# Value tiles 1 to 3 as three rounded products, with their upper and lower parts made by ScalarE, GpSimd and VectorE

## The reference, cut to what matters

```python
z = x @ w_in                                  # columns: pool 256, q 384, k 384, v 384, ssm 384
y_pool = pool_mixer(u_pool, ...)              # trailing means of 2, 4, 8, 16 tokens, then a small product
y_attn = chunk_attention(q, k, v, rel_bias)   # 6 heads of 64, softmax over own and previous chunks
y_ssm  = s5_mixer(u_ssm, ...)                 # state space, GELU, then y * sigmoid(y @ w_glu + b)
heads  = concat(rmsnorm(y_pool), rmsnorm(y_attn), rmsnorm(y_ssm))
h      = layer_norm(ALPHA * x + heads @ w_out)
x      = layer_norm(ALPHA * h + moe(h) + sigmoid(h @ w_ple_gate) * (p @ w_ple_proj))
```

## Time and profile before

| what | value |
|---|---|
| time of the kernel, median of 3 runs | 428.99 us (428.87 to 429.12) |
| time of the profiled execution | 429.05 us |
| its span in the trace | 427.3 us |
| PE, PEld, DVE, ACT, POOL busy | 413.3, 238.1, 255.4, 129.6, 93.6 us |
| mean granted TensorE clock | 0.993 |
| DMA, mean over the span | 240 GB/s |

### The profile page before, as it was taken

The page is one execution under the profiler, slowest core; times in us unless marked ns, Lnnn a source line. Parts: engine busy times, 40 slices in busy tenths (PEclk is TensorE's granted clock), DMA queues, the critical chain, the costliest instruction groups (busy, mean ns, idle before and its releaser), DMA issues.

```text
span 427.3 us, 5594 instructions
## 1 busy us (share of the span) xinstructions
PE 413.3 (97%) x2167; PEld 238.1 (56%) x2167; DVE 255.4 (60%) x464; ACT 129.6 (30%) x235; POOL 93.6 (22%) x132
## 2 busy tenths in 40 slices
PE   8899999999999999999999999999999999999992
PEld 5677655469667555676577887333333433333271
DVE  2999985986873999998867524211101112224987
ACT  4721336025497890200621011011110111111243
POOL 2830269275000800000000742010111111000000
PEclk9999999999999999999999999999999999999997
DMA  7994103251997891111490428999999999977313
GB/s 264 431 397 129 49 2 66 68 130 51 276 411 295 285 392 63 49 49 51 158 384 8 191 43 325 425 410 413 418 417 418 421 411 411 423 289 247 152 45 153
DMA packets 33626, 102.76 MB, mean 240 GB/s; under 512 B 14882, under 2 KB 16082, under 8 KB 26816
## 3 DMA queue, kind: packets, MB, share of 16 engines
q1 hardware_dynamic: 26032, 92.79, 56.1%
q0 software_dynamic: 4016, 7.97, 5.6%
q10 hardware_dynamic: 3552, 1.65, 1.4%
HBM read 93.29 MB, written 15.24 MB: 254 GB/s over the span
## 4 chain that ended last, share of the span: by engine, by line
PE 67%; issue 23%; DVE 4%; DMA 3%; POOL 1%; ACT 1%; DVEq 0%; POOLq 0%; ACTq 0%
PE bank L1307 20%; PE bank L1317 10%; PE bank L952 7%; PE bank L1000 5%; PE bank L1302 3%; PE bank L967 3%; PE bank L992 3%; PE bank L1009 2%; PE bank L988 2%; PE bank L1067 2%; PE bank L1057 2%; POOL slot_scratch L595 1%; PE bank L995 1%; PE bank L1123 1%; PE bank L1122 1%
## 5 line engine op out<-in xcount | busy, mean ns | idle before, releaser
L1307 PE MATMUL bank<-region_a,region_g 128*64 128x512 f32 (+1 forms) x224 | 77.8, 594 | 0.0
L1317 PE MATMUL bank<-region_a,region_c 128*64 128x512 f32 (+1 forms) x160 | 43.7, 596 | 0.0
L1885 DVE TENSOR_TENSOR region_c<-region_c,bank 128x256 f32<-128x256 f32 x12 | 5.1, 421 | 64.6 <-ACT region_c L907 64.6
L1307 PE MATMUL bank<-region_h,region_g 128*64 128x512 f32 (+1 forms) x96 | 42.4, 594 | 0.0
L1307 PE MATMUL bank<-region_b,region_g 128*64 128x512 f32 (+1 forms) x96 | 42.4, 594 | 0.0
L1307 PE MATMUL bank<-region_c,region_g 128*32 128x512 f32 (+1 forms) x96 | 42.4, 594 | 0.0
L1878 DVE COPY region_g<-bank 128x512 f32<-128x512 f32 x24 | 15.5, 687 | 40.4 <-PE bank L1302 40.4
L1307 PEld LDWEIGHTS bank<-region_a,region_g 128*64 128x64 f32 (+1 forms) x224 | 22.2, 123 | 25.1 <-issue 24.4
L1151 PE MATMUL bank<-region_b,region_e 128*128 128x512 f32 x68 | 32.9, 607 | 0.0
L907 ACT ACTIVATE region_c<-bank 128x256 f32<-128x256 f32 x12 | 4.6, 384 | 83.9 <-PE bank L1307 83.9
L952 PE MATMUL bank<-region_e,region_a 128*128 128x512 f32 x64 | 28.0, 595 | 0.0
(11 more groups left out here) (364 smaller groups left out, 881.9 us busy)
## 6 DMA issues: line engine op xcount, KB each, us to landing
region_a<-in_w_exp_down SPq DMA_DIRECT2D x10, 1024.0 KB, 14.4
region_a<-in_w_exp_gate SPq DMA_DIRECT2D x7, 1024.0 KB, 8.4
region_a<-in_w_exp_up SPq DMA_DIRECT2D x7, 1024.0 KB, 12.1
region_b<-in_w_out SPq DMA_DIRECT2D x1, 4096.0 KB, 14.7
expert_scratch<-zero_scratch SPq DMA_DIRECT2D x8, 512.0 KB, 9.5
region_c<-in_w_ple_gate SPq DMA_DIRECT2D x2, 1536.0 KB, 23.1
region_b<-in_w_exp_gate SPq DMA_DIRECT2D x3, 1024.0 KB, 10.3
region_b<-in_w_exp_up SPq DMA_DIRECT2D x3, 1024.0 KB, 12.3
```

The lines of the kernel that those rows point to most:

```text
L1307: return mm(out_[at:at + width].rearrange("p (u n) -> p u n", u=2), x[:, k, at:at + width], w[:, k], start=(k == 0), stop=(k == KD - 1), t ...
L1317: return mm(bank[banks[half]][at:at + width, :], act_e[:, r, 2, k * P + at:k * P + at + width], w[:, k, half * 512:half * 512 + 512], star ...
```

## The change

Value tile 0 stays as it was. Tiles 1 to 3 become `v_split`: 24 float32r matmuls each (upper x by upper w, lower x by upper w, upper x by lower w, eight blocks each) in place of eight float32 ones. For that:

- ACT makes the upper parts of `w_v` (2304 and 768 columns) and of all of x (2560 and 1536 columns) between its copies of the projections and `v_copy(0)`.
- POOL makes the lower part of x in two instructions (2560 and 1536 columns), in the middle of its trailing sums, and DVE the lower part of `w_v` in two (2304 and 768), behind `row_max(3)`. Both lowers are written over the originals, so both wait for value tile 0.
- `scores(2)` on PE moves ahead of the state products, `add_bias` and `row_max` of heads 4 and 5 on DVE ahead of `normalise(2)`, and `exps(4)` on ACT ahead of `v_copy(1)` and the `pt_copy`s.
- The upper parts lie in free places of regions a, b, c and f. The part of `w_o` from block 6 on, the first piece of `w_pg` and `xh` are loaded there later, so SP now waits for the last value tile between `w_o`'s first six blocks and the rest; `xh` goes behind the first piece of `w_pg`.

```diff
 V_BANKS = (6, 7, 2, 5)
+XV_PARTS, WV_PARTS = ((0, 5), (5, KD)), ((0, 6), (6, KD))
 PM_BANKS = (7, 0)
...
+        F0 = R0 + 4 * 4096
+        XV_AT, WV_AT = (F0 + 4 * 1536, B0 + 4 * 6656), (C0 + 4 * 768, A0 + 4 * 13440)
+        xv_hi = [over(f"value_input_upper{i}", (hi - lo) * T, XV_AT[i]) for i, (lo, hi) in enumerate(XV_PARTS)]
+        wv_hi = [over(f"value_weights_upper{i}", (hi - lo) * ATT_W, WV_AT[i]) for i, (lo, hi) in enumerate(WV_PARTS)]
+        xv_lo = over("value_input_lower", KD * T, R0)
+        wv_lo = over("value_weights_lower", KD * ATT_W, A0 + 4 * O_V)
+
         pp_hi = over("ple_proj_upper", 2 * D, G0 + 4 * 2048)
...
             for m in range(3):
-                load(yT[:, m, :].rearrange("p (j c) -> p j c", j=CH), y_d.rearrange("j f c -> f j c")[m * P:(m + 1) * P], "y_back")
+                load(yT[:, m, :].rearrange("p (j c) -> p j c", j=CH), y_d.rearrange("j f c -> f j c")[m * P:(m + 1) * P], "y_out")
...
             sp.wait_ge(S["rot_ready"], 3)
-            load(w_o, io["w_out"].rearrange("(k p) n -> p k n", p=P), "wo_in")
-
+            w_o_v = io["w_out"].rearrange("(k p) n -> p k n", p=P)
+            load(w_o[:, 0:6], w_o_v[:, 0:6], "wo_in")
+            sp.wait_ge(S["pe_v"], NT)
+            load(w_o[:, 6:KD], w_o_v[:, 6:KD], "wo_in")
+
+            w_pg_v = io["w_ple_gate"].rearrange("(p k) n -> p k n", k=KD)
+            load(w_pg[:, 0, 0:6], w_pg_v[:, 0:6, 0:512], "wpg0_in")
             sp.wait_ge(S["s_read"], HEADS)
             load(xh, io["x"].rearrange("(t p) d -> p t d", p=P), "xh_in")
-
-            w_pg_v = io["w_ple_gate"].rearrange("(p k) n -> p k n", k=KD)
-            load(w_pg[:, 0, 0:6], w_pg_v[:, 0:6, 0:512], "wpg0_in")
             sp.wait_ge(S["pool_ready"], 1)
...
             add_shift(b2, a, 2, 64, slice(0, 1))
+            gp.wait_ge(S["xw_hi_set"], 12)
+            gp.wait_ge(S["pe_v"], 1)
+            for (lo, hi), upper in zip(XV_PARTS, xv_hi):
+                at = slice(lo * T, hi * T)
+                g.tensor_tensor(xv_lo[:, at], RE[:, at], upper[:], ALU.subtract).then_inc(S["gp_lo_set"], 1)
+            gp.wait_ge(S["gp_lo_set"], 2)
             link(g.tensor_copy(a[64:P, 0:1], b2[64:P, 0:1]))
...
             qk_copy(5)
+
+            def value_weights_upper(i):
+                at = slice(O_V + WV_PARTS[i][0] * ATT_W, O_V + WV_PARTS[i][1] * ATT_W)
+                a.activation(wv_hi[i][:], RA[:, at], ACT.Copy).then_inc(S["xw_hi_set"], 1)
+
+            ac.wait_ge(S["wv_in"], 32)
+            value_weights_upper(0)
             pool_copy(1)
+            value_weights_upper(1)
+            ac.wait_ge(S["s_ready"], 1)
+            for (lo, hi), upper in zip(XV_PARTS, xv_hi):
+                a.activation(upper[:], RE[:, lo * T:hi * T], ACT.Copy).then_inc(S["xw_hi_set"], 1)
             ac.wait_ge(S["wglu_in"], 16)
...
                 y_copy(m)
+            exps(4)
             v_copy(1)
...
             pt_copy(1)
-            exps(4)
             exps(5)
...
                 a.activation(hd_hi[k][:], hdT[:, k, P:T], ACT.Copy).then_inc(S["wo_hi_set"], 1)
-            ac.wait_ge(S["wo_in"], 16)
+            ac.wait_ge(S["wo_in"], 32)
             for k in (0, 1, 5, 6, 7):
...
+            def v_split(t, bank_i):
+                pe.wait_ge(S["xw_hi_set"], 12)
+                pe.wait_ge(S["gp_lo_set"], 2)
+                pe.wait_ge(S["xw_lo_set"], 10)
+
+                def upper(parts, homes, width, k, at, w):
+                    i = 0 if k < parts[0][1] else 1
+                    first = (k - parts[i][0]) * width + at
+                    return homes[i][:, first:first + w]
+
+                for term in range(3):
+                    for k in range(KD):
+                        x = xv_lo[:, k * T + t * P:k * T + t * P + P] if term == 1 else upper(XV_PARTS, xv_hi, T, k, t * P, P)
+                        w = wv_lo[:, k * ATT_W:(k + 1) * ATT_W] if term == 2 else upper(WV_PARTS, wv_hi, ATT_W, k, 0, ATT_W)
+                        last = mm(bank[bank_i][:, 0:ATT_W], x, w, start=(term == 0 and k == 0), stop=(term == 2 and k == KD - 1))
+                last.then_inc(S["pe_v"], 1)
+
             def scores(pair):
...
             v_tile(0, V_BANKS[0])
+            pe.wait_ge(S["s_read"], 4)
+            scores(2)
...
                 last.then_inc(S["pe_y"], 1)
-            pe.wait_ge(S["s_read"], 4)
-            scores(2)
...
             pe.wait_ge(S["y_evac"], 1)
-            v_tile(1, V_BANKS[1])
+            v_split(1, V_BANKS[1])
             turn_probs(0)
             turn_probs(1)
-            v_tile(2, V_BANKS[2])
+            v_split(2, V_BANKS[2])
             turn_probs(2)
             turn_probs(3)
-            v_tile(3, V_BANKS[3])
+            v_split(3, V_BANKS[3])
             turn_probs(4)
...
-            pe.wait_ge(S["wo_in"], 16)
+            pe.wait_ge(S["wo_in"], 32)
             pe.wait_ge(S["pool_mixed"], 2)
...
             row_max(3)
+            dv.wait_ge(S["xw_hi_set"], 10)
+            dv.wait_ge(S["pe_v"], 1)
+            for (lo, hi), upper in zip(WV_PARTS, wv_hi):
+                tt(wv_lo[:, lo * ATT_W:hi * ATT_W], RA[:, O_V + lo * ATT_W:O_V + hi * ATT_W], upper[:],
+                   ALU.subtract).then_inc(S["xw_lo_set"], 1)
+            add_bias(4)
+            add_bias(5)
+            row_max(4)
+            row_max(5)
             normalise(2)
...
             tt(wg_lo[:], w_glu.rearrange("p k n -> p (k n)"), wg_hi[:], ALU.subtract).then_inc(S["glu_lo_set"], 1)
-            add_bias(4)
-            add_bias(5)
-            row_max(4)
-            row_max(5)
-            dv.wait_ge(S["y_back"], 48)
+            dv.wait_ge(S["y_out"], 96)
             for m in range(3):
```

More of the change, by code:

```diff
@@ L309, in trunk @@
             "kern_in kern_done rot_ready xrot_done "
-            "u_out u_back m0_in s_ready s_moved y_evac y_out y_back yin_ready gelu_done glu_lo_set glu_sig ssm_done "
+            "u_out u_back m0_in s_ready s_moved y_evac y_out gp_lo_set yin_ready gelu_done glu_lo_set glu_sig ssm_done "
             "pool_ready pool_mixed pe_u pe_qk pe_pool pe_v pe_bxT pe_kern pe_x pe_s pe_pt pe_pv pe_pm pe_y "
```

## The result

The changed kernel takes 430.09 us (median of 12 runs, 429.76 to 431.55) against 428.98 us for the kernel before in runs beside it: 1.0026 times the time of before, interval 1.0018 to 1.0034. That is 1.1 us slower. The forecast was 427.7 us and its range ended at 429.7. The profiled execution took 430.32 us, its span is 428.6 us and its mean granted clock 0.991 (before 0.993).

A forecast was written before the change was run, and what follows sets the result against it. PE was taken as the bound. Tiles save 3.3 us, but tile 1's saving and 0.8 us are lost to a wait: gated product at 131.00 + 0.8 - 1.06 - 1.06 = 129.7; 429.05 - 1.3 = 427.75, say 427.7, range 426.4 to 429.7.

The forecast's parts named there:

- Tile 2 then ends at 120.4: PE, value tile 2: starting at 116.3 and taking 4.1 us, it ends at 120.4.
- the step before it: PE ahead of head 1's transposes: waits from 113.0 to 115.0 for ACT, so tile 2 starts at 116.3.
- at about 117.7: DVE reaches the state products for the skip term then; hidden, wait ahead of head 3's transposes stays 0.2 us.
- gain = 1.3 - (t - 106.1): Gated product's start: 1.3 us earlier if DVE finishes `w_v`'s lower part at 106.1, changing one for one with t.
- The second rival: POOL's splits slower (2.2 ns, t 107.1, gain 0.3) or matmuls bound by weight loads (gain 0.4); around 428.7; chance 0.17.
- the prediction's own sum: Lower parts alternating: POOL 94.7 to 99.7, DVE to 102.25, POOL to 105.25, DVE to 106.1.
- The first: POOL and DVE lower parts don't hold each other up: DVE through at 99.7, gated product 2.0 us early, 427.0; chance 0.2.
- The late gate piece: Gate piece lands late behind SP's wait: at the 14.7 us bound DVE starts 3.2 us late, 430.45; chance 0.1.
- The last one: All 3.3 us from the three value tiles arrive, DVE never late at either transposes, 425.8; chance 0.05.

The follow-up runs named there:

- The fills: Throwaway matmuls in PE's wait: changed kernel plus 14 (431.06 us) or 12 (431.15); changed kernel with head 4's exponentials behind the copies, plus 22 ahead of head 3's transposes (429.94).
- the kernel with the bias first: Changed kernel with DVE's lower part of `w_v` behind the bias and maxima of heads 4 and 5; 428.08 us, 0.9986.
- The kernel with the fill: Changed kernel plus 14 throwaway float32r matmuls on PE between the transposes of heads 0 and 1; 431.06 us, 1.0040.
- the last experiment: Bias and head 4's division moved first in the changed kernel, POOL's remaining sums held for that division, its two last also for the skip term; 426.21 us, 0.9939.
- the kernel with the division first: Changed kernel with bias and maxima ahead of `w_v`'s lower part, plus head 4's division ahead of the skip term; 427.65 us, 0.9968.

## Why the prediction was wrong

**The step that failed** is "Tile 2 then ends at 120.4". It put 4.1 us, the time at the upper clock level, behind a PE wait that the step before it had itself put at 2 us, and charged the wait once. Tile 2 took 5.83 us, 1.57 us more than tile 1. The fills show the cause: with PE kept busy, the tile takes 4.28 us, and where the wait was moved to head 3 the fill gave 1.3 us back in the time of the kernel. What is shown here is the price of a wait of 2.79 us. For one of 2.0 us as forecast it may be nothing: the wait of 2.05 us in the kernel with the bias first left the clock at 1.00. The trace of the kernel before had no row for this price: up to 420 us PE never waits longer than 1.32 us in it and the granted clock is 1.00. Only behind PE's last matmul does it fall, to 0.50 from 423 us on.

**A second step failed behind it**, and it weighs more. DVE starts the skip term at 119.59, not "at about 117.7". Of the 1.9 us, 0.8 is the late t (the time at which DVE is through with the lower part of `w_v`), and about 1.0 is `normalise(2)`, 3.11 us beside POOL's sums where 1.27 plus 0.8 had been allowed. The kernel with the fill shows what that costs, 1.33 us ahead of head 3's transposes in place of 0.2. In the changed kernel the slow tile 2 hides it. So with the clock's loss taken away only 0.4 of the 2.7 us that were missed come back; every kernel here that is faster than before has DVE's stream rearranged.

**The sum, again, with what was measured.** The gated product began 2.7 us later than forecast (132.38 against 129.7). By the chain, from whose rows the forecast was added up, tile 2 started 1.06 us late (117.36 against 116.3), took 1.54 us more than 4.1 (5.64), and tile 3 took 0.09 more (4.19). Of the 1.06, 0.8 is the late t, 106.9 against 106.1; "gain = 1.3 - (t - 106.1)" holds nearly as far as the start of tile 2, and not behind it.

**Terms that were mis-sized.** POOL's column costs 2.2 ns in this operation, not 1.95: 9.04 us for 4096 columns undisturbed. The forecast took the rate of one of POOL's additions, 1.89 us for 1022 columns, as the nearest row, and read the 2.48 us of its last sum as partly waiting. The other sum of 1024 columns stands in the same timeline of the kernel before:

```profile
97.10 2.36 POOL L573 TENSOR_TENSOR region_c<-region_c 128x1024 f32<-128x1024 f32 x1
```

That is 2.30 ns a column, and in the last experiment the two sums take 2.38 and 2.41 us. So at most 0.1 us of the 2.48 was waiting, and the rate of these two would have put t at about 107.5, an estimate by the prediction's own sum. The second rival had 2.2. The Trainium skill (GPSIMD Engine Reference, section 3.1) has about 2.6 cycles a column, 2.2 ns; the measurement agrees with it for this instruction. A tile is 4.26 us from start to start, 178 ns a matmul, not 171.

**What was right.** DVE and POOL alternate, instruction by instruction, and 2304 columns have 6.7 us (about 6 forecast) and 768 have 4.2 (3.9). The Trainium skill's rule for the shared port pair (SBUF — State Buffer, section "SBUF: two separate sides"), that one engine holds it for a whole instruction and the other is blocked, is borne out by the kernels in which POOL waits: the same divisions take 1.27 us or 2.2 to 3.2. Tile 1 doesn't wait. The wait comes back ahead of head 1's transposes, released by ACT, 2.79 us for a forecast 2.0. Head 3's wait stays 0.22, but by luck: the slow tile 2 gave DVE the time that it lacked. The loads are hidden: DVE takes the gate piece at 141.34 without a wait. And what the gated product has lost or won reaches the end: +1.4 there, +1.3 in the span; in the last experiment -2.9 at the gated product and in the time (the fills in the first wait apart, whose loss at 259 us is open).

**The rivals.** The first is refuted by DVE's 10.8 us. The second, POOL slower, happened, with t at 106.9 for its 107.1, but it was priced at a gain of 0.3 us, no change: it too left out the clock. The late gate piece didn't happen. The last one, all of the tiles' saving, is what the kernel with the two POOL waits comes near to: 2.9 of 3.3 us at the gated product (three tiles at 4.26 us save 2.9).

## What to carry to other kernels

Price a wait on TensorE twice: once for its length, and once for the clock behind it. Here waits of 2.8 to 4.1 us cost 1.4 to 1.6 us more, and waits of 2.05 us and less nothing; where the trace before has no such wait, the second price belongs into the range. When work is split over VectorE and GpSimd, list every instruction of both in time order and reckon with their alternating; the ones that nobody waits for (here the trailing sums) are to be held back by a semaphore until the other engine has room. And when one wait is removed, look for the same late engine at the next place that it serves: moving the exponentials back only moved the wait from head 1 to head 3.

## What the runs showed of the hardware

- The granted clock fell to 0.50 behind PE waits of 2.79, 4.02 and 4.13 us, and the work behind them took 1.57, 1.4 and 1.6 us longer than at the upper level. It did not fall behind waits of 2.05, 1.81 and 1.33 us. So the 0.8 us that DVE came late may have decided whether the clock fell at all; no run has this wait at other lengths in the same place, and that stays open.
- Three VectorE instructions with two on-chip inputs of 512 columns went from 2.07 to 7.17 us beside three GpSimd instructions of 504, 1024 and 1024 columns: each of them waited for a GpSimd instruction to end. GpSimd is held up in the same way: in the kernel with the division first, its copy of 512 columns takes 3.84 us beside VectorE's two lower parts of `w_v`, and 0.61 in the kernel before.
- Not everything on VectorE is held up. Six copies out of PSUM take 3.15 us beside the two 1024-column sums of the last experiment (L1708), as in the kernel before without them; the eight row maxima take 3.22 us beside a 1024-column sum in the changed kernel, and 3.23 undisturbed.
- 24 float32r matmuls of 384 columns take 4.26 us, eight float32 ones took 5.16 to 5.37.
